# Eight modulation groups beside the first projection, softmax weights divided on GpSimd, delta-rule gates inside the short convolution

## What is computed

```python
ml = jnp.split(silu(c) @ ada_w[layer] + ada_b[layer], 6)        # and mc from c_ctx
a_lat = rms_norm(h_lat, norm1_w) * (1 + ml[1]) + ml[0]
# first network, attention: three dilations joined, causal, ALiBi bias
p = exp(scores + bias - max);  o = (p / sum(p)) @ v
# second layer of the second network
q, k, v, g, a_in, b_in = split(a @ w_in)                        # 3104 columns
q, k, v = silu(conv3(q)), silu(conv3(k)), silu(conv3(v));  q, k = l2norm(q), l2norm(k)
log_a = -exp(a_log) * softplus(a_in + dt_bias);  beta = sigmoid(b_in)
o = gated_delta_rule(q, k, v, log_a, beta)    # chunks of 64, both directions
```

## Time and profile before

| | us |
|---|---|
| timed runs, three | 3078.76, 3078.95, 3080.92 |
| their median | 3078.95 |
| the profiled execution | 3074.76 |
| its span, first to last instruction | 3073.0 |
| TensorE busy | 2806.8 (91%) |
| VectorE, ScalarE, GpSimd busy | 1146.3, 915.6, 402.9 |

### The profile page before, as it was taken

One profiled execution on the slowest core, in us unless ns is written; L12 is line 12 of the kernel. 1 busy time (PEld: TensorE's weight loads), 2 busy tenths in 40 slices (PEclk: granted clock), 3 DMA queues, 4 the chain that ended last, 5 costly groups with the idle time before them and its releaser, 6 DMA issues. The chain is left out here.

```text
span 3073.0 us, 50216 instructions
## 1 busy us (share of the span) xinstructions
PE 2806.8 (91%) x21568; PEld 2084.8 (68%) x21568; DVE 1146.3 (37%) x1643; ACT 915.6 (30%) x1522; POOL 402.9 (13%) x340
## 2 busy tenths in 40 slices
PE   8988869999999798999999999998896788799999
PEld 6654555444444676646778888887685677678887
DVE  3133452222223513554353333234243455454333
ACT  3223321111111213335331212123264445432222
POOL 0011030000000600135200000000001556200001
PEclk9999889999999899989999999999897899999999
DMA  4259727999995111010112121211211000223331
GB/s 155 82 186 345 280 100 271 393 391 391 395 391 227 62 52 65 1 50 1 56 55 61 63 68 55 68 62 34 100 42 35 4 4 4 83 84 95 96 98 65
DMA packets 223264, 389.56 MB, mean 127 GB/s; under 512 B 9471, under 2 KB 100506, under 8 KB 222586
## 3 DMA queue, kind: packets, MB, share of 16 engines
q1 hardware_dynamic: 145578, 198.40, 19.0%
q10 hardware_dynamic: 77520, 188.75, 16.3%
HBM read 381.36 MB, written 5.77 MB: 126 GB/s over the span
## 5 line engine op out<-in xcount | busy, mean ns | idle before, releaser
L2002 PE MATMUL ps<-mlp_h_low,mlp_w_high 128*128 128x512 f32 (+1 forms) x768 | 272.0, 354 | 0.0
L2002 PE MATMUL ps<-mlp_h_high,mlp_w_high 128*128 128x512 f32 (+1 forms) x768 | 271.9, 354 | 0.0
L2002 PE MATMUL ps<-mlp_h_high,mlp_w_low 128*128 128x512 f32 (+1 forms) x768 | 271.6, 354 | 0.0
L1856 ACT ACTIVATE mlp_w_high<-mlp_ring 128x2048 fp32r<-128x2048 f32 x64 | 122.2, 1912 | 316.2 <-PE ps L2002 316.2
L2002 PE MATMUL ps<-mlp_x_low,mlp_w_high 128*128 128x512 f32 (+1 forms) x576 | 204.0, 354 | 0.0
L2002 PE MATMUL ps<-mlp_x_high,mlp_w_high 128*128 128x512 f32 (+1 forms) x576 | 203.9, 354 | 0.0
L2002 PE MATMUL ps<-mlp_x_high,mlp_w_low 128*128 128x512 f32 (+1 forms) x576 | 203.7, 354 | 0.0
L254 POOL TENSOR_TENSOR aT<-aT 128x512 f32<-128x512 f32 (+1 forms) x30 | 59.6, 1985 | 1029.7 <-ACT aT L246 1029.1
L1860 DVE TENSOR_TENSOR mlp_w_low<-mlp_ring,mlp_w_high 128x2048 fp32r<-128x2048 f32 x64 | 146.5, 2292 | 62.8 <-ACT mlp_w_high L1856 62.8
L2002 PEld LDWEIGHTS ps<-mlp_h_high,mlp_w_high 128*128 128x128 f32 x768 | 145.3, 189 | 20.4
L2066 DVE SCALAR_TENSOR_TENSOR hT<-ps,mod,hT 128x512 f32<-128x512 f32 x96 | 63.5, 662 | 256.0 <-PE ps L2002 256.0
(11 more groups left out here) (557 smaller groups left out, 5932.2 us busy)
## 6 DMA issues: line engine op xcount, KB each, us to landing
mlp_ring<-in_mlp_w_dram SPq DMA_DIRECT2D x64, 1024.0 KB, 5.3
e_wg<-in_w_gate_dram ACTq DMA_DIRECT2D x15, 4096.0 KB, 15.6
e_wu<-in_w_up_dram ACTq DMA_DIRECT2D x15, 4096.0 KB, 15.1
ring<-in_w_down_dram ACTq DMA_DIRECT2D x15, 4096.0 KB, 13.8
ring<-in_ada_w_dram SPq DMA_DIRECT2D x24, 2048.0 KB, 9.8
ring<-in_w_in_dram SPq DMA_DIRECT2D x6, 2048.0 KB, 7.6
proj_ring<-in_even_w_in_dram SPq DMA_DIRECT2D x8, 1024.0 KB, 5.3
odd_room<-in_gdn_w_in_dram SPq DMA_DIRECT2D x8, 1024.0 KB, 5.2
```

Of the source, the lines that this page charges most:

```text
L1856: act.activation(self.high[:, slot], self.ring[:, slot], ACT.Copy).then_inc(self.w_high, 1)
L2002: last = pe.matmul(bank(st, n, s, b - a), w[:, st % 2, k, n * P:(n + 1) * P], x[:, k, a:b], start=(k == 0 and p == 0), stop=(k == KT - 1 a ...
```

## The change

- **Modulation.** Groups 0 to 7 (`FIRST = 8`) are multiplied in `proj1`, after units 4, 5, 7, 8, 10, 11, 13 and 14. They are fetched into the memory of `H.f`, `H.i`, `H.gate` and `H.key`, which are written only by later units; `proj1` uses seven banks, since bank 7 collects the modulation. The clearing and the silu of the condition move there too. In `dilated` groups 8 to 15 are multiplied, in the first two units of each head pair.
- **Softmax weights.** No diagonal any more: GpSimd multiplies the exponentials by the inverted sums in place, and TensorE turns the result with plain transposes against the identity. The pipeline is one unit deeper (turning at t - 2, values at t - 3) with three buffers of weights. GpSimd's products of the recurrence are spread between the divisions. ScalarE copies a turned unit before it takes the next exponentials.
- **Gates.** `chunk_gates` becomes a class `ChunkGates`, whose steps stand in `short_conv`: the small transfers behind `proj3`'s, the store first on SP in the convolution, matmuls after tiles 0 and 2, ScalarE's parts at n = 1 and 4, VectorE's at 1, 2, 3 and 5.
- **Norms and keys.** Items are normalised from tile 6 on (q first, then k), key transposes are at tiles 14 and 15 and, four groups, after the last tile; the second block of transposes goes.
- **Masks.** `delta`'s six transfers are issued at the end of the convolution's SP list.

```diff
@@ gemm
+            if stream:
+                stream.fetch(sp, 0)
+                stream.fetch(sp, 1)
             for j, job in enumerate(jobs):
                 if j < slots:
                     continue
+                if stream:
+                    for g in stream.fetches(ends[j - slots - 1] if j > slots else 0, ends[j - slots]):
+                        stream.fetch(sp, g)
                 sp.wait_ge(full, ends[j - slots])
...
                 last.then_inc(full, 1)
+                if stream:
+                    stream.beside(pe, u)
...
+                if stream and me == "act" and u == 1:
+                    stream.silu(eng)
@@ Modulation
+    UNITS = (4, 5, 7, 8, 10, 11, 13, 14)
+    def fetches(self, first, last):
+        return [g for g in range(2, FIRST) if first <= self.UNITS[g - 2] < last]
+    def beside(self, pe, u):
+        if u in self.UNITS:
+            self.multiply(pe, self.UNITS.index(u))
@@ dilated
+        group_of = lambda u: FIRST + 2 * (u // 4) + u % 4
...
+                def divide(t):
+                    pool.wait_ge(inverted, t + 1)
+                    p = sc[:, t % 3, :, 0:L_of(t)]
+                    pool.tensor_tensor(p, p, inv[:, t, :].unsqueeze(2).to_broadcast([P, 2, L_of(t)]), ALU.mult).then_inc(divided, 1)
...
+                for t in range(n + 2):
+                    if t < n:
+                        divide(t)
+                    j, r = t // 4, t % 4
+                    if r == 2:
+                        low(j)
+                    if r == 3:
+                        end_keys(j)
+                    if r == 0 and j:
+                        in_keys(j - 1)
+                    if r == 1 and j:
+                        queries(j - 1)
...
-                        pe.wait_ge(exped, 2 * (u + 1))
-                        pe.wait_ge(scaled, 2 * (u + 1))
+                        pe.wait_ge(divided, u + 1)
...
-                                last = pe.matmul(E.bank(4 + h2)[:, k * P:(k + 1) * P], sc[:, u % 2, h2, k * P:(k + 1) * P], diag[:, u % 2, h2, :],
-                                                 start=True, stop=True)
+                                last = pe.transpose(E.bank(4 + h2)[:, k * P:(k + 1) * P], sc[:, u % 3, h2, k * P:(k + 1) * P], E.ident)
                         last.then_inc(turned, 1)
+                        if i < 2:
+                            stream.multiply(pe, group_of(u))
...
-                        dve.wait_ge(inverted, t + 1)
-                        for h2 in range(2):
-                            dve.tensor_scalar(diag[:, t % 2, h2, :], E.ident, inv[:, t, h2:h2 + 1], None, ALU.mult).then_inc(scaled, 1)
@@ short_conv
+                gates.store(sp)
                 for g in range(2, tiles // 2):
                     sp.wait_ge(w_low, 2 * (g - 1))
                     sp.dma_start(ring[:, g % 2], conv_weight(w, g)).then_inc(loaded[g % 2], 16)
+                constants.fetch(sp)
...
+                    if n == 0:
+                        gates.logits(pe)
+                    if n == 2:
+                        gates.sums(pe)
-                    if n >= 8:
-                        e, T = n - 8, items[n - 8][1]
+                    if AHEAD <= n < AHEAD + 8:
+                        e, T = n - AHEAD, items[n - AHEAD][1]
...
+                    if n >= tiles - 2:
+                        pe.wait_ge(used, 8)
+                        if n == tiles - 1:
+                            pe.wait_ge(keys_out, 1)
+                        turn_keys(2 * (n - tiles + 2), 7)
+                pe.wait_ge(padded, tiles - 1)
+                for i in range(4):
+                    turn_keys(2 * (i + 2), i + 2)
...
+                    if n == 1:
+                        gates.logs(act)
+                    if n == 4:
+                        gates.decays(act)
+                    if n == tiles:
+                        for i in range(2, 6):
+                            act.wait_ge(turned, i + 1)
+                            act.activation(own[:, 512 * i:512 * i + 512], E.bank(i), ACT.Copy)
```

More of the change, by code:

```diff
@@ L618, in _ @@
                 normed.beside(pool)
+        if stream:
+            @block.gpsimd
+            def _(pool):
+                stream.clear(pool)
 def kn(w):
@@ L846, in attention_and_hgrn @@
         H = Parts()
-        H.q, H.f, H.i, H.gate, H.key = (sb(f"h_{n}", [P, 4, S]) for n in ("q", "f", "i", "gate", "key"))
+        H.q, later = sb("h_q", [P, 4, S]), sb("h_rest", [P, 2, KT * S])
+        H.f, H.i, H.gate, H.key = (later[:, i // 2, 4 * S * (i % 2):4 * S * (i % 2 + 1)].rearrange("p (n t) -> p n t", n=4) for i in range(4))
         w = d["w_in"][0]
@@ L850, in attention_and_hgrn @@
         opening(E, ring)
+        stream = Modulation(E, c, later, room)
         ahead = c.enter_context(ExitStack())
@@ L872, in attention_and_hgrn @@
                           group(2, "t", V, None), group(3, "f", H.q, silu(H.q)), group(4, "f", H.f, forget),
-                          group(5, "t", H.i, None), group(6, "f", H.gate, silu(H.gate))], ahead=ring, normed=normed)
+                          group(5, "t", H.i, None), group(6, "f", H.gate, silu(H.gate))], banks=7, ahead=ring, normed=normed,
+             stream=stream)
         ahead.close()
-        stream = Modulation(E, c, room)
+        stream.rows = sb("ada_rows", [P, 512])
         H.dec, H.attn = sb("hg_dec", [P, 4, S // 32]), sb("dil_o", [P, 4, S])
@@ L2796, in odd_mixer @@
         gate, ab = room[:, 0:KT * S].rearrange("p (k t) -> p k t", k=KT), room[0:32, KT * S:KT * S + TT]
+        own = E.aT[:].rearrange("p k t -> p (k t)")
+        gates = ChunkGates(E, G, gate, ab, gate_dram, own[:, 3072:])
+        constants = Constants(E, sb("gdn_U", [P, 2, 64]), sb("gdn_eye", [P, 64]))
         c2 = c.enter_context(ExitStack())
@@ L2806, in odd_mixer @@
                                  for a, b in ((0, S), (S, TT))])],
-             ahead=ring, normed=normed, then_fetch=conv.fetch)
-        chunk_gates(E, G, gate, ab, gate_dram)
-        own = E.aT[:].rearrange("p k t -> p (k t)")
+             ahead=ring, normed=normed, then_fetch=lambda sp: gates.fetch(sp, conv, normed))
         G.kt = own[:, 0:NCH * 256].rearrange("p (c j a n) -> p c j a n", c=NCH, j=2, a=2)
@@ L2918, in conv_weight, with short_conv @@
 def conv_weight(w, g):
     return kn(w[:, 256 * g:256 * (g + 1)])
-def short_conv(E, w, q, k, vc, xh, xl, ring, own):
+def short_conv(E, w, q, k, vc, xh, xl, ring, own, gates, constants):
     nc, d, sem = E.nc, E.d, E.sem
-    tiles = 16
+    tiles, AHEAD = 16, 6
     piece = lambda t: t.rearrange("a (c n) -> a c n", n=64)
-    items = [(k[:, :, p % 2, p // 2, :], TT, 1.0) for p in range(4)] + [(piece(q[:, p, :]), S, 64.0) for p in range(4)]
+    items = [(piece(q[:, p, :]), S, 64.0) for p in range(4)] + [(k[:, :, p % 2, p // 2, :], TT, 1.0) for p in range(4)]
@@ L2947, in _, with turn_keys @@
                     sp.dma_start(ring[:, g % 2], conv_weight(w, g)).then_inc(loaded[g % 2], 16)
+                constants.fetch(sp)
             @block.tensor
             def _(pe):
+                def turn_keys(m, bank):
+                    for i, (ch, j) in enumerate((ch, j) for ch in (m, m + 1) for j in range(2)):
+                        last = pe.transpose(E.bank(bank)[:, i * P:(i + 1) * P], k[:, ch, j].rearrange("a g t -> a (g t)"), E.ident)
+                    last.then_inc(turned, 1)
                 for n in range(tiles):
@@ L3030, in _ @@
                         last.then_inc(out, 1)
-                    if 8 <= n < tiles:
-                        root(n - 8)
+                    if AHEAD <= n < AHEAD + 8:
+                        root(n - AHEAD)
             @block.gpsimd
```

332 lines of the change are left out of this document (175 added, 157 removed).

## The result

The changed kernel takes 3047.21 us (median of four runs, 3039.6 to 3056.0) against 3079.43 for the kernel before: ratio 0.9895, 95% interval 0.9873 to 0.9918, so some 32 us less, where 46 were forecast (3033 us, in a range of 3016 to 3052). A second set gave 0.9887 (0.9842 to 0.9931). The profiled execution took 3050.03 us with a span of 3047.8, only 24.7 less than the profiled execution of before. The windows of both profiles, cut where the stages begin, say where.

What follows compares the result with a forecast made beforehand. TensorE was taken to bound the first projection and DMA the attention. Gains of 18.4 us (parts 1 and 2) and 27.4 (part 3) sum to 45.8: 3078.95 - 45.8 = 3033 us, range 3016 to 3052.

Steps and rivals of the forecast that it cites:

- Part 1: First projection: eight of 24 modulation weight groups multiplied beside it, on a full TensorE, 15.4 us lost.
- Part 2: Attention without its DMA bound: 33.8 us gained there, 18.4 net of the projection's loss.
- The pair: Attention: one head pair takes 15 us (bounds 12 and 18), set by the chain between VectorE's reductions and ScalarE's exponentials.
- The rival of GpSimd: Attention: GpSimd or DMA sets the pace, 18 us a pair, about 3043 us in all; chance 0.17.
- that of half clock: Attention: TensorE stays at 1.2 GHz and becomes the bound, 24 us more, 3057; chance 0.07.
- The lock term: Attention: VectorE waits for the port pair it shares with GpSimd, 1.0 us added to each head pair.
- Part 3: Second layer: gates beside the convolution, with norms, key transposes and masks moved, 27.4 us gained.
- The logits' price: Convolution: the gates' small matmuls behind tiles 0 and 2 cost 4.1 us of TensorE at full clock.
- my third rival: Convolution: small matmuls pull the clock down twice, 5 us more, and tail or delta rule keeps 4: 3042; chance 0.10.
- The sums: Convolution: the gates' sums on TensorE, their input made by VectorE behind its taps, cost 0.3 us.
- The value transposes: Convolution's tail: the clock should hold after a 2.7 us pause, 2.4 us gained (bounds 0 and 2.9).
- First sums of the delta rule: Start of the delta rule: its first sums run at full clock, 1.0 us gained (bounds 0 and 5).

Runs made afterwards that it cites:

- the later set: Stage readings of two kernels: parts 1 and 2 with the old odd layer (74.4 us; whole 3065.66 us, 0.9949) and the changed kernel repeated unaltered (74.6; 3043.77 us, 0.9887).
- the doubled divisions: Projection and attention changes with the old odd layer, plus a second GpSimd product of the same size behind each division: 3064.71 us, ratio 0.9957, stage 77.0 us.

## Why the prediction was right, and where not

- **The time, right, and in part by the width of the range.** 3047 lies 14 us above the 3033 of the sum and inside 3016 to 3052.
- **Bound of the kernel before, right.** TensorE full in the one stage, DMA in the next: with the new softmax alone nothing moved (0.9996), with the modulation alone all of it came.
- **Part 1, right.** 16.7 us lost for 15.4: a multiplication cost 2.1 us (16.7 / 8) and not the 1.92 of its own row. None waited for weights.
- **Part 2, the time right, its ground only in part.** Forecast 72.0 us for the stage, measured 71.3, and in the later set 74.4 and 74.6. Groups 8, 10 and 11 waited and no later one. Units 8, 12 and 15 came at 245.2, 259.0 and 272.5, where the sum has 244.7, 259.7 and 273.2 with the 16.7 us of part 1. The pair, 15 us in the sum, took 14.85 to 14.88 at the end of three profiles, and 13.05 when its chain was shortened: the chain named was the one that bound. (The terms behind unit 0 of a pair add up to 2.4, not 2.7; that changes nothing.) The rival of GpSimd falls with the doubled divisions (2.6 to 5.7 us for 21), that of half clock with 0.86 to 0.93 in the stage. The lock term was right in kind and short in size, 1.5 for 1.0. By the rule of the Trainium skill (SBUF — State Buffer, "SBUF: two separate sides") an instruction of VectorE that has two inputs in SBUF, or runs in a two-port mode, waits out the whole instruction of GpSimd that holds their shared ports; the copy at 828 ns for 176 agrees, and that not every one waits kept the price under the 2 us a division that the rule alone would allow. What I did not see is that the old softmax would have done as well. Its diagonals took VectorE 10.8 us in the profile of the modulation alone, 2.7 a pair; the lock beside the divisions took 1.5 a pair back. That this is why the pair is hardly shorter is an argument, no run separates the two.
- **Part 3, 26.4 forecast without the delta rule's first sums, 21.6 in the pair of profiles** (16.6 - 8.2 + 13.2). The block 16.6 for 16.7, the silu 3.3, the masks 6.1 for 6.4: right. Three steps failed. The logits' price: 4.0 us themselves, as forecast, but tile 1 behind them ran at half clock, 3 more; that was the condition of my third rival, at 0.10, and a third of its 9 us came, with one fall of the clock and not two. (The row itself ran at full clock, so the 0.50 of the earlier trace rows was not the doing of small matmuls alone: TensorE was idle for half of that stretch.) The sums took 1.2 (2192.64 to 2193.85) for 0.3: seven instructions of 48 or 96 columns, fourteen passes, are not nothing. The value transposes: 7.10 us, so 0.95 gained of 2.4. They began at full clock, but it was at half by 2314.2 and for some 3 us, behind a pause of 2.78 us, where I had read from the earlier trace rows that it holds up to 3.18. One row was too little for a limit; what had gone before each wait may count, which no run here tells apart.
- **First sums of the delta rule, 1.0: not to be seen.** Its stage was 296.7 to 304.7 us in six profiles with the old start and 297.7 to 304.8 in eight with the new odd layer.
- **"Nothing behind either stage is a fixed date, so the shift reaches the end": wrong as to one execution.** Everything behind does shift, but unchanged stages differ from one execution to the next by up to 12.8 us. That is the larger part of the gap between 45.8 and the 24.7 of the pair of profiles (12.8 of 21.1; part 3 has 4.8, the delta rule 1.9, the attention 0.5, small changes elsewhere 1.1), and the sum had no term for it. Against the ratio (32 us less) about 5 of the 14 missing are part 3's; the rest can't be told from the scatter.

## What to carry to other kernels

Where DMA is full in one stage and idle in the next, move transfers over, and subtract what their work costs the engine that is full there (here 16.7 us of TensorE). But try the move alone first: here it gave all, and the softmax that was rewritten for it nothing. Small matmuls stood best in one row ahead of a stage that began at half clock anyway, worse in a row behind its first tile, and worst between large ones. To compare two versions of a pipeline, take its repeat in steady state (14.85, 14.87, 14.88 us a pair) and not the stage (71.3 to 74.6). And before a missing 10 us is explained, compare stages whose code did not change: two profiles of one kernel may differ by as much.

## What the runs showed of the hardware

- TensorE busy without a gap can stay at 1.2 GHz: 30.16 of 31.00 us busy and a granted clock of 0.50, with a large matmul and four small passes in turn (the stretch began at half clock, behind a pause of 3.12 us). It had 2.4 GHz within 6 us of the last small one.
- Two executions of one kernel can be granted different clocks for the same work. The even layer's matmuls (most of 64 to 512 columns), TensorE 84 and 85 us busy of 90, were granted 0.71 in one execution of the changed kernel and 0.87 in another of the same kernel at nearly the same place of the program. The windows, first execution, then second (which holds more of the program, as it runs faster):

```profile
1262.00:1352.00 90.00, 83.92 (x382) 55.99 (x382) 30.42 (x36) 19.00 (x32) 15.07 (x10) 0.71 0.06 20
```

```profile
1264.30:1354.30 90.00, 85.28 (x420) 52.59 (x419) 36.75 (x45) 19.02 (x32) 18.85 (x13) 0.87 0.06 20
```

- A VectorE copy of sixteen columns took 176 ns with GpSimd's divisions absent and 828 beside them.
- The same DMA-bound stage ran at 348 to 375 GB/s in four profiles of the old attention (110.4, 106.9, 105.9 and 101.7 us).
